# Where the state rotations are built, when the second mixer's matrices are fetched, and how long one accumulator bank is held, in a five-layer fp32 block on one core

## The reference, cut to what matters

```python
def _s5_mixer(h, w_in, log_dt, lambda_re, lambda_im, ...):
    u, z = jnp.split(h @ w_in, 2, axis=-1)
    dt = jnp.exp(log_dt)[:, None]
    mag = jnp.exp(lre * dt)
    ab_re = mag * jnp.cos(lim * dt)
    ab_im = mag * jnp.sin(lim * dt)
    ...
    # x[t] = ab * x[t-1] + bb * u[t]   (complex, 64 groups of 64 states)
    # y[t] = Re(c * x[t]) + d * u[t]
    y = jax.nn.gelu(y.reshape(bsz, seq, SSM_WIDTH))
    ga, gb = jnp.split(y @ w_glu, 2, axis=-1)
    y = ga * jax.nn.sigmoid(gb) * jax.nn.silu(z)
    return y @ w_out
```

## Time and profile before

| | |
|---|---|
| median of 3 runs | 1976.67 us (1976.65 to 1977.06) |
| the profiled execution's own time | 1976.76 us |
| its span in the trace | 1974.9 us |
| mean granted TensorE clock | 0.968 of full speed |
| busy: PE, DVE, ACT, POOL | 1830.2, 968.0, 853.2, 194.4 us |

### The profile page before, as it was taken

One profiled execution on the slowest core, in us unless ns is written; L12 is line 12 of the kernel. 1 busy time (PEld: TensorE's weight loads), 2 busy tenths in 40 slices (PEclk: granted clock), 3 DMA queues, 4 the chain that ended last, 5 costly groups with the idle time before them and its releaser, 6 DMA issues.

```text
span 1974.9 us, 24065 instructions
## 1 busy us (share of the span) xinstructions
PE 1830.2 (93%) x9758; PEld 1464.3 (74%) x9758; DVE 968.0 (49%) x1622; ACT 853.2 (43%) x1437; POOL 194.4 (10%) x318
## 2 busy tenths in 40 slices
PE   6899999699889999997999999999899789999996
PEld 4677777479878877875687777877787568888884
DVE  7878456454754354244345445345544454344223
ACT  6445666445354234234345553355623443222222
POOL 2000226710000000000000000022200021111000
PEclk9999999899999999999999999999999879999998
DMA  4554331035142323311232222211132112232331
GB/s 134 171 185 132 100 107 44 1 102 202 65 155 85 101 82 116 96 44 43 84 93 70 84 70 91 89 64 64 54 100 86 61 64 97 95 103 87 99 93 57
DMA packets 60319, 181.29 MB, mean 92 GB/s; under 512 B 7008, under 2 KB 18080, under 8 KB 57776
## 3 DMA queue, kind: packets, MB, share of 16 engines
q1 hardware_dynamic: 60208, 179.75, 28.0%
HBM read 165.57 MB, written 16.25 MB: 92 GB/s over the span
## 4 chain that ended last, share of the span: by engine, by line
PE 73%; DVE 11%; ACT 7%; POOL 4%; issue 2%; DMA 1%; SPq 0%; DVEq 0%; ACTq 0%; POOLq 0%
PE bank L886 18%; PE bank L887 17%; PE bank L888 17%; PE bank L925 2%; PE bank L927 2%; PE bank L926 2%; DVE wlo L1906 2%; PE bank L1067 1%; POOL Ps L2661 1%; ACT Ps L1804 1%; PE bank L1088 1%; ACT whi L1357 1%; ACT L1362 1%; PE bank L906 1%; PE bank L908 1%
## 5 line engine op out<-in xcount | busy, mean ns | idle before, releaser
L1906 DVE TENSOR_TENSOR wlo<-wraw,whi 128x1024 fp32r<-128x1024 f32 (+1 forms) x262 | 316.7, 1211 | 332.2 <-ACT whi L1357 330.9
L886 PE MATMUL bank<-Hh,whi 128*128 128x512 f32 (+2 forms) x1104 | 446.3, 404 | 16.4 <-DVE wlo L1906 16.3
L887 PE MATMUL bank<-Hl,whi 128*128 128x512 f32 (+2 forms) x1104 | 435.0, 394 | 0.0
L888 PE MATMUL bank<-Hh,wlo 128*128 128x512 f32 (+2 forms) x1104 | 434.8, 394 | 0.0
L1357 ACT ACTIVATE whi<-wraw 128x1024 fp32r<-128x1024 f32 (+1 forms) x262 | 271.5, 1040 | 313.1 <-PE bank L888 239.7
L886 PEld LDWEIGHTS bank<-Hh,whi 128*128 128x128 f32 (+2 forms) x1104 | 208.6, 189 | 75.0 <-DVE wlo L1906 14.1
L888 PEld LDWEIGHTS bank<-Hh,wlo 128*128 128x128 f32 (+2 forms) x1104 | 208.5, 189 | 46.8 <-issue 0.6
L887 PEld LDWEIGHTS bank<-Hl,whi 128*128 128x128 f32 (+2 forms) x1104 | 208.6, 189 | 45.4 <-issue 2.2
L1362 ACT ACT_TABLE_LOAD x97 | 124.5, 1283 | 2.8 <-DVE epst L1921 1.1
L886 PE MATMUL bank<-Bh,whi 128*128 128x512 f32 x256 | 103.5, 404 | 2.2 <-DVE Bl L2435 2.2
L887 PE MATMUL bank<-Bl,whi 128*128 128x512 f32 x256 | 102.6, 401 | 0.0
(11 more groups left out here) (360 smaller groups left out, 3064.2 us busy)
## 6 DMA issues: line engine op xcount, KB each, us to landing
wraw<-in_w_o SPq DMA_DIRECT2D x24, 512.0 KB, 3.4
wraw<-in_w_bgate SPq DMA_DIRECT2D x24, 512.0 KB, 3.4
wraw<-in_w_branch SPq DMA_DIRECT2D x24, 512.0 KB, 3.4
wraw<-in_w_fg SPq DMA_DIRECT2D x22, 512.0 KB, 3.4
wraw<-in_w_fu SPq DMA_DIRECT2D x22, 512.0 KB, 3.5
wraw<-in_w_glu SPq DMA_DIRECT2D x16, 512.0 KB, 3.5
wraw<-in_w_fd SPq DMA_DIRECT2D x16, 512.0 KB, 3.5
scratch_CA<-CA SPq DMA_DIRECT2D x4, 1152.0 KB, 6.2
```

Source lines behind the costliest of these rows:

```text
L886: pe.matmul(o, wh[:, cols], hi(k), start=k == 0, stop=False)
L887: pe.matmul(o, wh[:, cols], lo(k), start=False, stop=False)
L888: m = pe.matmul(o, wl[:, cols], hi(k), start=False, stop=k == K - 1)
L1906: dve.tensor_tensor(c.wlo[q][:, 0:n], c.raw[i % RR][:, 0:n], c.whi[q][:, 0:n].bitcast(F32), S_).then_inc(*up(DID, ("wlo", i)))
```

## The change

Three edits.

1. `prep_r` now does only m = 0 to 3, on GpSimd, at loop steps 28, 30, 32, 34. The doublings m = 4 and m = 5 become 18 single VectorE instructions of 128x512 (`prep_r_wide(part, n)`, 3 parts of 6), one at each of the loop steps 38 to 55. The 18 GpSimd operations that did this are gone.
2. `w2` and `w3` stand earlier in the written order (behind s0 and s1), `m2` behind o0, and `m3` behind o1.
3. Bank `("kk", b)` is given back at step `prep_w(b, 1, 2)` and not at once.

```diff
@@ attention @@
-            if i >= AWAY + 6 and (i - AWAY) % 4 == 2 and (i - AWAY - 6) // 4 < 6:
-                self.step("prep_r", (i - AWAY - 6) // 4)
+            if i in range(AWAY, AWAY + 8, 2):
+                self.step("prep_r", (i - AWAY) // 2)
+            if i in range(AWAY + 10, AWAY + 28):
+                self.step("prep_r_wide", *divmod(i - AWAY - 10, 6))
@@ prep @@
             self.step("prep_k", b)
-            self.bank.give(("kk", b))
             for n in range(3):
                 self.step("prep_w", b, 1, n)
                 if n == 2:
                     self.step("store_k", b)
+                    self.bank.give(("kk", b))
                 yield
@@ s5 @@
-        order = ("a0 b0 m1 a1 e0 b1 r0 a2 s0 b2 r1 a3 s1 r2 b3 w2 o0 s2 z0 r3 t0 o1 w3 m2 z1 s3 y0 t1 z2 o2 m3 y1 z3 t2 "
+        order = ("a0 b0 m1 a1 e0 b1 r0 a2 s0 w2 b2 r1 a3 s1 w3 r2 b3 o0 m2 s2 z0 r3 t0 o1 m3 z1 s3 y0 t1 z2 o2 y1 z3 t2 "
                  "o3 y2 z4 t3 y3 z5 z6 z7")
@@ vector @@
+    def prep_r_wide(part, n):
+
+        w, b0, b1 = [(16, 0, 4), (32, 0, 2), (32, 2, 4)][part]
+        R = lambda i, n0, n1: c.Rh[:, b0:b1, i, :, n0:n1]
+        last = lambda i: c.Rh[:, b0:b1, i, :, w - 1:w].broadcast_to([128, b1 - b0, 8, w])
+        t1, t2 = [x[:, :].rearrange("p (b q n) -> p b q n", q=8, n=w) for x in c.tR]
+        on.wait_ge(*at("Rs"))
+        if n in (0, 3):
+            tt(t1, R(0, 0, w), last(n // 3), M)
+        elif n in (1, 4):
+            tt(t2, R(1, 0, w), last(1 - n // 4), M)
+        else:
+            tt(R(n // 5, w, 2 * w), t1, t2, A_ if n == 5 else S_, *([("Rh",)] if (part, n) == (2, 5) else []))
```

More of the change, by code:

```diff
@@ L2545, in vector @@
                     norm0=norm0, ev=ev, gate_t=gate_t, cmp_out=cmp_out, soft_in=soft_in, soft_out=soft_out,
-                    na=na, nb=nb, nc=nc, nd=nd, prep=prep, prep_b=prep_b, prep_ca=prep_ca, prep_w=prep_w,
+                    na=na, prep_r_wide=prep_r_wide, nb=nb, nc=nc, nd=nd, prep=prep, prep_b=prep_b, prep_ca=prep_ca, prep_w=prep_w,
                     store_k=store_k, split_g0=split_g0, split_h1=split_h1, s5_in=s5_in, rsS=rsS, rows=rows, states=states,
@@ L2606, in prep_r @@
                 gp.tensor_copy(c.Rh[:, :, i, :, 0], c.e8[:, i, :].rearrange("p (b q) -> p b q", b=4)).then_inc(*up(DID))
[L2607 to L2616, removed]
+        R = lambda i, n0, n1: c.Rh[:, :, i, :, n0:n1]
+        last = lambda i: c.Rh[:, :, i, :, n - 1:n].broadcast_to([128, 4, 8, n])
+        t1, t2 = [x[:, 0:32 * n].rearrange("p (b q n) -> p b q n", q=8, n=n) for x in c.tR]
+        rot(t1, R(0, 0, n), last(0), M)
+        rot(t2, R(1, 0, n), last(1), M)
+        rot(R(0, n, 2 * n), t1, t2, ALU.subtract)
+        rot(t1, R(0, 0, n), last(1), M)
+        rot(t2, R(1, 0, n), last(0), M)
+        rot(R(1, n, 2 * n), t1, t2, ALU.add, *([("Rs",)] if m == 3 else []))
     def bias(t, a):
```

## The result

The changed kernel takes 1944.2 us (median of four runs, 1942.74 to 1945.44) against 1976.66 us before (four runs beside it, 1974.23 to 1977.06). The ratio is 0.9838, 95% interval 0.9821 to 0.9855: faster by 32.4 us (28.7 to 35.4). The forecast was 1942.7 us. The profiled execution took 1944.1 us, with a span of 1942.1 against 1974.9 us.

A forecast was written before the change was run, and what follows sets the result against it. TensorE was taken as the bound (73% of the chain that ended last), so edits pay only where it stands still. Gains 12.9 + 15.2 + 6.0 = 34.1 us off 1976.76 gave 1942.7 us, range 1938 to 1947, or 1934 to 1953 including rivals A, B, C.

The forecast's parts named there:

- 1a: Attention steps 32 to 63: with doublings off GpSimd and free, four stretches take 68.4 us against 93.4, gaining 25.0.
- 1b: First attention stretch: small doublings exceed GpSimd's idle time, stalling TensorE 5.4 us, rounded up to 5.9; stretch 23.0 us.
- The upper bound of 24.5 us: First attention stretch: each of the two long waits also costs 1.4 us of slow clock.
- 1c: Second and third attention stretches: eight products make VectorE the bound at 18.5 us, meetings with scalings add 1.7; 20.2 each.
- rival A: Middle attention stretches: the VectorE-GpSimd lock costs in full, 24.0 us per stretch, 1950.3 us in total; chance 0.17.
- 2, the fetches: Second mixer: earlier fetches remove waits before `states(2)` and `outputs(3)` and the slow clock behind; 15.2 us gained.
- late next: Second mixer: ScalarE and VectorE are late next, `turned(2)` already waiting 0.29 us for `Yo`; 0.6 us come back.
- 3, the bank: Preparation: the 4.43 us wait for `Kp` goes, with the slow clock behind it; 6.0 us gained.
- B: Attention: products fit VectorE's idle time and small doublings mostly GpSimd's; gain 20.3, total 1935.3 us; chance 0.15.
- C: Second mixer gives back half, the VectorE scan, `zy`, ScalarE `Yo` chain standing behind the waits; 1950.3 us; chance 0.08.
- D: Attention steps 40 to 55: short pauses keep TensorE at 1.2 GHz, 27 us per stretch, leaving 20 gained; chance 0.02.
- E: Second mixer: the fetches don't move because a bank or buffer holds `states(2)`; 1950; chance 0.02.

The follow-up runs named there:

- the products left out: The changed kernel with 12 of the 18 VectorE products left out and six replaced by writes of a constant; 1935.76 us against 1975.91.
- spread_b: The changed kernel with small doublings at steps 28, 34, 36, 44 and products at steps 46 to 67, none at the two 384-wide steps of each eight; 1934.72 us.
- the repeated run: The changed kernel itself, unaltered, run again beside the others; 1942.84 us, ratio 0.9828.
- spread_a: The changed kernel with small doublings every fourth step (28, 32, 36, 40) and products from step 42 to 65, none at the two 384-wide steps; 1940.71 us.
- spread_d: spread_b with the m = 3 doubling cut into three operations at step 42 and three at step 44; 1934.57 us.
- spread_e: spread_d with the products three, one and two at a time at steps whose number modulo 8 is 3, 5 and 7; 1935.56 us.
- only two moved: The kernel before with only the fetches w2 and w3 moved, m2 and m3 left in place; ratio 0.9948, 10.3 us less.
- the bank alone: The kernel before with only the later giving back of bank kk; ratio 0.9966, 6.7 us less.
- the rotations alone: The kernel before with only the two hunks on `prep_r` and `prep_r_wide`; ratio 0.9951, 9.7 us less.

## Why the prediction was right, point by point

**1a and the frame.** "Were all of them free, 68.4 against 93.4": with the products left out the last three stretches take 17.2, 17.8 and 16.9 us, with spread_b the first 17.1. The floor of 17.1 was right.

**1b, the small doublings.** Forecast stalls 1.1 + 1.9 + 2.4 and a first stretch of 23.0 us; measured 1.10, 1.53 and 1.14 (0.68 + 0.46), and 22.62. The third is smaller because TensorE was at 1.2 GHz just ahead of it (clock 0.50 from 321.5 to 323.0 us) and had less to wait for. So 3.8 us of stalls and 1.7 us of other loss, most of it the slow clock, stand where I had 5.4 and 0.5. In the repeated run the stalls were 1.09, 1.50 and 2.73, which is the forecast, at a clock of 1.00, and the stretch was as long (23.6 for 23.7 in the table). The method, a doubling's length minus the idle time ahead of the next scalings, gave the 1.1 us of m = 1 in a slot that I had not seen (spread_a), but missed what else m = 3 held up there. The upper bound of 24.5 us for this stretch does not follow from its own terms: 17.1 + 5.4 + 2 x 1.4 is 25.3. Nothing hangs on it.

**1c, the products.** Forecast 18.5 for VectorE plus 1.7 for the meetings, 20.2 us; measured 21.24 and 20.69, so 1.5 us too little for both, offset by 0.4 and 0.7 us in the first and fourth. That 80.5 us came so near to 80.9 is luck to that extent. The size was near, the reason only in part. One sign that I had named for being right did not come: TensorE's waits for `Pl` were to be 5 to 7 us, all before step 40. They are 10.2 us, 6.5 of them behind it. I took VectorE as the bound once its busy time passed TensorE's 16.4 us. But it still has 2.4 us of idle in 20.7. What TensorE waits for is one chain, z tile to `stp`, once in eight steps. With the two steps ahead of it left free (spread_b, spread_d) a product costs 0.33 us instead of 0.45 (2.0 us for six against 3.6 for eight, over 17.1), and with three in a row ahead of it (spread_e) 0.5 to 0.6 (3.1 and 3.5 us for six). The meetings hit GpSimd more than VectorE: 0.4 to 0.5 us a group of scalings, 0.87 in the group of width 512 that meets two products, and on a product 0.06 us on the mean (0.75 for 0.69).

**1c, who shuts out whom.** By the Trainium skill ("SBUF — State Buffer", section "Who interferes with whom") a VectorE instruction with two SBUF inputs and a GpSimd instruction that reads SBUF contend for one shared port pair, which is an exclusive lock. The trace agrees: the single scaling at 350.29, beside a product of 0.69 us that had just started, took 1.09 us for 0.57. That the length of a scaling is then lost on VectorE's chain each time, rival A, was not seen. A group is four scalings of 0.57 to 0.67 us each, and no product in the middle stretches took more than 0.93 us, which is a wait of 0.24. By the same section an instruction with one SBUF input does not contend, outside the two-port modes, and a multiplication by a constant can enter such a mode. The one of the experiment took 0.51 us for the elements that take a product 0.69, so it may have run in such a mode; no run here shows whether it did, and the 0.2 us don't speak against the exception.

**2, the fetches.** Forecast 8.7 + 7.1 - 0.6 = 15.2, measured 15.75. Up to the start of `outputs(3)` 8.76 with only two moved, where the forecast had 8.7 - 0.6; 0.9 us of waits for `Yo` instead of 0.29 are the "late next" that was named. The steps were right one by one, also that no weight load is held up: SyncE issued `mW` at 482.05 and 497.20, and TensorE waited for no `wlo` from 440 to 600 us.

**3, the bank.** Forecast 6.0, measured 6.20 and in the bank alone 6.23.

**The rivals.** A: products above 1 us and 24 us per stretch; not seen. B: 18.5 us and all fits into idle time; the idle time was there, but not at the slots chosen: spread_d comes to 72.9 in the table and 0.8 behind it, near B's sum of 73.1. C: no wait of TensorE above 0.5 us in the second mixer. D: the clock in the two middle stretches is 1.00, and 0.93 and 0.92 in the repeated run, which cost it nothing that shows. E: the fetches moved.

**The total.** 34.1 us forecast, 34.4 by the marks, 32.4 between the medians. The 2.0 us between the last two lie inside the interval of the timed gain (28.7 to 35.4), and the traces show no term of the sum that would have failed by that much; scatter of this kind the forecast had not put a size on, term by term.

## What to carry to other kernels

Before moving work onto another engine, list that engine's and its neighbours' idle gaps in one period and put each piece where the gap ahead of the next released instruction is longer than the piece: in regular slots the 18 products and the small doublings cost 13.6 us, in chosen ones 5.3 (82.0 against 68.4; 72.9 against 68.4 and 0.8 behind the table). Most of the difference came from the slots of the doublings, which are longer than the gaps that they stood in. Leave a distance, too, between a piece and the first instruction that needs its result: an in-order queue stops there (2.52 us in spread_a). An engine's busy share does not tell this; the chain from its last gap to the instruction that releases the next engine does. Fetches for a later stage that wait behind an unrelated step in one queue are worth their wait and the slow clock behind it, and both can be read off ahead.

## What the runs showed of the hardware

The clock behind a wait is not fixed by the wait. The same wait of TensorE for `wlo`, 2.13 us after (it ends at 417.90) and 2.12 us before (at 435.34), and the 6 us around it (stretch, length, busy, clock, DMA share, GB/s), after:

```profile
415.00:421.00 6.00, 3.87 (x13) 0.81 0.31 102
```

and before:

```profile
432.50:438.50 6.00, 3.88 (x18) 1.00 0.33 102
```

Eight matmuls took 0.63 us each in the one and 0.40 in the other, which costs 1.5 us. The wait of 2.18 us that ends at 297.36 in the kernel before was followed by 1.2 GHz, and the same wait after, 2.19 us to 293.82, was not. The row of before holds the wait, the one of after begins right behind it:

```profile
294.00:300.00 6.00, 3.82 (x28) 0.82 0.00 0
```

```profile
294.00:300.00 6.00, 5.96 (x58) 1.00 0.01 3
```

Six such waits of 2.0 to 3.4 us stand ahead of 450 us outside the edited stretches, in all 13 traces with nearly the same lengths. The mean granted clock in the 6 us behind each, over these traces (0.72 to 0.76 means that a part of them ran at 1.2 GHz):

| wait, us | ends, in the trace after | 0.72 to 0.76 | 0.92 to 0.95 | 1.00 |
|---|---|---|---|---|
| 3.4 | 55.56 | 9 | 4 | 0 |
| 2.6 | 72.79 | 13 | 0 | 0 |
| 2.0 | 87.48 | 4 | 0 | 9 |
| 2.4 | 115.14 | 13 | 0 | 0 |
| 2.2 | 293.82 | 6 | 0 | 7 |
| 2.1 | 417.90 | 3 | 0 | 10 |

So two of the six cost the same in every trace, and the others cost up to about 1.5 us more in one trace than in another. Nor is it all chance between runs. The slow clock at 417.90 stands in both traces of the changed kernel and in the rotations alone, and in none of the ten others: it may be a price of the rotations' edit that the forecast had no term for. Behind the wait at 293.82 the clock was full in seven of the eight traces with all three edits, and in none of the five with fewer. No run tests why. That such steps of 1.5 us make up most of the scatter between runs of one kernel (3.7 us for the kernel before, 5.5 for spread_d), and what the three single gains missed when added up, is an inference; no run tested it by itself.
